# Third attention of a three-layer transformer kernel: another share of gate pieces for each step

## The reference, cut to what matters

```
for each of 8 heads (2 groups of keys, 4 heads each):
    o_c = softmax(q . kc) @ vc        # 31 compressed blocks of keys
    o_s = softmax(q . ks) @ vs        # selected keys: here all of the causal ones
    o_w = softmax(q . kw) @ vw        # window of 256 keys
    o   = g0 * o_c + g1 * o_s + g2 * o_w
out = sigmoid(x @ w_gate_mla) * (o_mla @ w_o_mla) + sigmoid(x @ w_gate_nsa) * (o_nsa @ w_o_nsa)
```

## Time and profile before

| | |
|---|---|
| median of 3 runs | 2529.7 us |
| profiled execution | 2527.73 us, span 2525.9 us |
| PE busy | 2501.9 us, 99% of the span |
| DVE busy | 1386.6 us, 55% |
| ACT busy | 941.4 us, 37% |
| mean granted TensorE clock | 0.998 |
| the NSA attention with its pieces | 1964.4 to 2095.5 us of the span |

### The profile page before, as it was taken

How to read it: one execution, slowest core, us unless ns; L and a number is a source line. 1 busy time by engine, 2 the same in 40 slices (tenths; PEclk the granted TensorE clock), 3 DMA queues, 4 the chain that set the end, 5 groups by cost and what they waited for, 6 DMA issues and landing times.

```text
span 2525.9 us, 29885 instructions
## 1 busy us (share of the span) xinstructions
PE 2501.9 (99%) x11809; PEld 2024.9 (80%) x11809; DVE 1386.6 (55%) x1902; ACT 941.4 (37%) x1359; POOL 60.3 (2%) x77
## 2 busy tenths in 40 slices
PE   9999999999999999999999999999999999999999
PEld 7788888888888877888888888888777658888887
DVE  6556366644556655545664454666655566733433
ACT  5432334322234443223342233445534564422222
POOL 6000000000000000000001000000000001000000
PEclk9999999999999999999999999999999999999999
DMA  4122223444443322222244333222222111222222
GB/s 164 67 84 98 85 100 108 149 143 150 149 143 108 104 67 77 91 101 91 101 142 136 132 104 131 100 92 94 100 101 71 47 34 67 100 100 98 94 91 100
DMA packets 38627, 260.02 MB, mean 103 GB/s; under 512 B 4416, under 2 KB 4672, under 8 KB 8048
## 3 DMA queue, kind: packets, MB, share of 16 engines
q1 hardware_dynamic: 32976, 226.92, 26.4%
q10 hardware_dynamic: 5296, 30.20, 3.4%
q0 software_dynamic: 240, 1.28, 0.2%
HBM read 256.29 MB, written 2.10 MB: 102 GB/s over the span
## 4 chain that ended last, share of the span: by engine, by line
PE 94%; DVE 3%; ACT 1%; issue 1%; DMA 0%; SPq 0%; DVEq 0%; ACTq 0%
PE ps L2043 65%; PE ps L2070 9%; PE ps L2278 6%; PE ps L2096 5%; PE ps L2220 2%; PE ps L2262 2%; PE ps L2242 1%; DVE w_lo L1166 1%; PE ps L2504 1%; PE ps L2520 1%; PE ps L2196 0%; PE ps L2560 0%; PE ps L2366 0%; DMA h<-x_t 0%; ACT pads L686 0%
## 5 line engine op out<-in xcount | busy, mean ns | idle before, releaser
L1166 DVE TENSOR_TENSOR w_lo<-raw,w_hi 128x2048 fp32r<-128x2048 f32 x208 | 477.6, 2296 | 325.0 <-ACT w_hi L598 275.1
L2043 PE MATMUL ps<-a_hi,w_hi 128*128 128x512 f32 x1408 | 550.5, 391 | 0.3 <-DVE w_lo L1166 0.3
L2043 PE MATMUL ps<-a_hi,w_lo 128*128 128x512 f32 x1408 | 547.9, 389 | 0.0
L2043 PE MATMUL ps<-a_lo,w_hi 128*128 128x512 f32 x1408 | 547.8, 389 | 0.0
L598 ACT ACTIVATE w_hi<-raw 128x2048 fp32r<-128x2048 f32 x198 | 376.5, 1901 | 404.2 <-PE ps L2043 338.3
L2043 PEld LDWEIGHTS ps<-a_hi,w_hi 128*128 128x128 f32 x1408 | 264.3, 188 | 56.8 <-issue 1.1
L2043 PEld LDWEIGHTS ps<-a_lo,w_hi 128*128 128x128 f32 x1408 | 264.4, 188 | 55.4 <-issue 1.0
L2043 PEld LDWEIGHTS ps<-a_hi,w_lo 128*128 128x128 f32 x1408 | 264.3, 188 | 55.0
L2043 PE MATMUL ps<-f_hi,w_hi 128*128 128x512 f32 x708 | 275.4, 389 | 0.0
L2043 PE MATMUL ps<-f_lo,w_hi 128*128 128x512 f32 x708 | 275.4, 389 | 0.0
L2043 PE MATMUL ps<-f_hi,w_lo 128*128 128x512 f32 x708 | 275.4, 389 | 0.0
(11 more groups left out here) (387 smaller groups left out, 3544.9 us busy)
## 6 DMA issues: line engine op xcount, KB each, us to landing
raw<-weights SPq DMA_DIRECT2D x209, 1024.0 KB, 4.8
ada_w<-ada ACTq DMA_DIRECT2D x24, 1024.0 KB, 4.9
merged<-cmp_w SPq DMA_DIRECT2D x2, 1024.0 KB, 5.9
out<-h SPq DMA_DIRECT2D x8, 256.0 KB, 2.0
h<-x_t SPq DMA_DIRECT2D x3, 512.0 KB, 7.2
raw<-weights SPq DMA_DIRECT2D x4, 256.0 KB, 5.2
kt<-c_row ACTq DMA_DIRECT2D x2, 512.0 KB, 3.4
pads<-p_t ACTq DMA_DIRECT2D x2, 512.0 KB, 4.1
```

What stands on the lines that cost most here:

```text
L1166: dve.tensor_tensor(w_lo[n % 2][:, w], raw[n % 2][:, w], w_hi[n % 2][:, w].bitcast(F32), ALU.subtract)\
L2043: ins = pe.matmul(dst, a[i], b[j], start=done == 0, stop=done == total - 1)
```

## The change

The list `share` is replaced. The order of the pieces, their number (48) and everything else stay.

```
-                share = [0] + [3, 2, 2, 1, 1, 1, 2] * 3 + [3, 3, 2, 2, 1, 1]
+                share = ([0, 3, 3, 2, 0, 2, 1, 2] + [3, 3, 2, 1, 2, 0, 2] + [2, 2, 2, 0, 2, 1, 1] + [2, 2, 0, 3, 3, 2])
```

## The result

| | before | after |
|---|---|---|
| median, of 5 runs each | 2529.74 us (2528.09 to 2530.45) | 2516.55 us (2515.53 to 2518.67) |
| ratio after / before, 95% interval | | 0.9949 (0.9935 to 0.9964) |
| profiled execution | 2527.73 us, span 2525.9 | 2517.49 us, span 2515.7 |
| first scores of the attention (line 2212) | 1964.43 | 1966.03 |
| first matmul of `out_nsa` (line 2070) | 2095.52 | 2085.31 |

A forecast was written before the change was run, and what follows sets the result against it. TensorE (PE), busy 99% of the span, was taken as the bound. 8.2 + 4.7 + 0.7 - 2.6 = 11.0 us off the 2529.7 us median forecast 2518.7 us; 8-in-10 range 2514.5 to 2524.0.

The forecast's parts named there:

- (a): PE's five waits for ScalarE's gate eviction, at the first pieces of tiles 1 to 5, all go: 8.2 us gained.
- (b): PE's two low-clock stretches, behind the waits at steps 9 and 23, go if those waits cause them: 4.7 us gained.
- the rival that rested on the rule: Clock falls elsewhere, behind new short waits in piece-free steps; one fall costs 3.4 us, giving 2522.1 us; chance 0.13.
- (c): Each group of pieces on PE costs 0.19 us beside its pieces; four groups disappear: 0.7 us gained.
- New waits: PE's waits where pieces no longer cover the chain through VectorE and ScalarE: 2.6 us added, bounds 0 and about 5.
- Steps 4 and 18: Without their piece, the next step's transposes wait for VectorE's weighing: 0.87 us added for each.
- Step 11: At full clock PE arrives sooner and waits for VectorE, which has low weights ahead of its mask: 0.35 us added.
- Steps 19 to 22: ScalarE's `w_hi` and VectorE's `w_lo` delay copies and masks once the gate wait goes: 0.3 us added, bound 1.2.
- The wait at step 9 stays: Tile 1's eviction comes late, so the 1.74 us wait and 3.4 us of low clock stay: 2523.8 us; chance 0.07.
- Cover counts more: New waits reach 5 us, with one clock fall: gain 5.2, 2524.5 us; chance 0.09 for larger waits or two falls.
- Hidden anyway: A later stage held by something other than PE gives the gain back: time stays 2529.7 us; chance 0.03.
- Slower: The clock falls behind every new wait, five places at 3.4 us each: 2535.7 us; chance 0.02.

The follow-up runs named there:

- 1: Changed kernel with the border at step 9 put back: tile 1 ends in the step where tile 2 begins; 2518.4 us, ratio 0.9957.
- 2: Kernel before with only the border at step 9 mended: step 8 has 4 pieces and ends tile 1; 2524.87 us, ratio 0.9988.
- 5: Kernel before with only the border at step 23 mended, tile 4 ending there and step 24 left empty; 2524.7 us.
- 6: Kernel before with only the border at step 23 mended, without an empty step, tile 5 beginning in step 24; 2523.29 us.
- 8: Changed kernel with only the border at step 23 put back (4 pieces there, 1 in step 25); 2522.69 us, ratio 0.9973.
- 3: Changed kernel with one piece given back as cover to steps 4 and 18, from steps 5 and 19; 2515.81 us, ratio 0.9951.
- 4: Changed kernel, same tile borders, with all empty steps but 24 filled with pieces from other steps; 2516.93 us, ratio 0.9954.
- 7: Changed kernel with one piece moved from step 5 to step 4 and one from step 10 to step 11; 2515.77 us, ratio 0.995.
- 11: Kernel 4's list, but with the weight-unit splits kept at steps 1, 9 and 19, as in the changed kernel; 2515.95 us, ratio 0.9944.
- 12: Kernel 4's list with weight-unit splits at fixed steps 1, 9 and 24, the third moved from step 19; 2514.22 us, ratio 0.9943.
- 9: Changed kernel with the borders at steps 9 and 23 both put back; 2522.87 us, ratio 0.9972.
- 10: Kernel before with its old list, but ScalarE's gate eviction placed ahead of the exponentials of step s+2; 2521.91 us, ratio 0.9974.

## Why the prediction was right

**(a) The gate waits: right.** 8.2 us forecast and 8.2 gone, the border at step 9 with it. Kernels 1, 2, 5, 6 and 8 show that each of the two borders within a step makes its own wait, and that this wait goes when the tile ends with its step. Slack at step 9 was put at 1.6 us and is 1.7.

**(b) The clock: right in this profile, as a mechanism only in part.** The step reads "if the low clock follows from the two long waits, both losses go with them: 4.7 us". In the stage there is no fall in any of the six kernels without a gate wait (after, 3, 4, 7, 11, 12), and every fall in the stage goes with one of the two long waits. (In before at tile 5 the clock is down from 2076.90, 0.3 us ahead of the end of the wait, and so before TensorE works again.) But the wait alone doesn't decide it. In the profiles, before's own included:

```
wait of PE            profiles with it            clock fell behind it
1.74 us, tile 2       before, 1, 5, 6, 9          before, 5, 6
2.4 to 3.5 us, tile 5 before, 2, 8, 9, 10         before, 8, 9, 10
0.55 to 1.23 us       13 waits (before, 2, 5, 6, 10)  none
```

A fall cost 1.7 or 3.4 us. So the two waits bring a chance of a fall in each execution, not a certain 4.7 us. The 62 executions of the kernel before in the four jobs show the same thing (mean granted clock, number, lowest, median and highest us):

```
0.996   6   2531.70   2532.27   2532.74
0.997  34   2528.61   2529.60   2531.46
0.998  16   2527.07   2527.88   2528.50
0.999   4   2525.68   2525.78   2526.55
1.000   2   2523.26             2523.35
```

The spread of 9.5 us between runs of one kernel goes with the clock. After's five runs are at 0.999 (2516.55 to 2518.67) and 1.000 (2515.53 and 2515.55). At 1.000 the difference of the kernels is 2523.3 - 2515.5 = 7.8 us, against 8.2 + 0.7 - 2.6 = 6.3 by the prediction's terms without the clock (7.4 with the sizes measured below). The rest of the 13.2 us, some 5 us, goes with the clock. This is rough: 0.001 of mean clock is 2.5 us of the span, and only two runs of each stand at 1.000.

The Trainium skill's rule (TensorE: Matmul & The Clock Gate, section "A second HAM failure mode: psum-queue depth-cycling"), by which short idles make the clock swing, is borne out in the stage for waits from 1.7 us, by 7 of 10 in the table. It is not for those up to 1.23 us there: neither the old gate waits nor the five waits of after, up to 0.95 us, brought a fall. But this is no length that holds everywhere. At the kernel's start, behind the wait of line 2162 at 25 to 26 us (the same work in all fourteen profiles), a fall of 1.7 us came in seven of them:

```
wait in us (profile it was in)
fall      0.92 (8)  1.16 (6)   1.39 (4)  1.63 (1)       1.67 (11)  1.81 (2)  1.83 (after)
no fall   0.83 (3)  0.87 (12)  1.03 (5)  1.25 (before)  1.32 (9)   1.43 (7)  1.61 (10)
```

PE's timeline there and the window behind it, of kernel 8:

```profile
25.13 1.05 PE L2162 MATMUL ps<-consts_sb,pads 128*128 128x1 f32 x8 [0.92 <-DVE pads L1238]
```

```profile
25.00:30.00 5.00, 4.87 (x19) 4.01 (x20) 3.25 (x12) 3.07 (x4) 4.42 (x8) 0.66 0.02 5
```

In the other direction, a wait of 1.5 us near 1791 us stands in all fourteen profiles and no fall follows it. So the rival that rested on the rule did not come in the stage, but the argument that I held against it, that 1.23 us or less brings no fall, does not hold for this kernel as a whole.

**(c) The price of a group: wrong.** 0.7 us were forecast and nothing came. The four steps that lost their group took as long as before, less the pieces and waits (the ledger of the stage). Kernel 7 confirms it: it has one group more than after, its waits are 0.67 us shorter, and its stage is 0.67 us shorter. The step counted a group from the start of its first piece, and did not look at what the transposes ahead of it cost when no piece follows.

**New waits: right in kind, 0.6 us too high.** Steps 4 and 18 cost 0.89 - 0.19 = 0.70 and 0.71 us. I had 0.87 each, since I counted the price of a group here too; without it PE arrives 0.7 us early. Step 11: 0.38 - 0.19 = 0.19 against 0.35. Steps 19 to 22: 0.22 against 0.3. Step 23: 0.21 against 0.2. Steps 13 and 24: 0, as said. Together 2.0 against 2.6.

**The sum.** 11.0 us were forecast for the profiled execution, and the stage gave 11.8. That it came so near is in part luck, since three wrong sizes offset each other. The 0.7 us of (c) did not come, and the new waits were 0.6 us too high by the same mistake. Left out was what a gate wait costs beyond its brackets, 0.22 to 0.26 us where it can be read (steps 5, 15 and 19; step 9 by kernel 1), an estimate of 1.2 us for five. For the clock 5.0 - 0.4 = 4.5 us are left, against 4.7. With these sizes the sum is 8.2 + 1.2 + 4.5 - 2.0 = 11.9. Then 1.6 us were lost again at the kernel's start, by a fall that the change has nothing to do with, so `out_nsa` starts at 2085.31 and not at 2084.5. The falls near 25 to 32 us are in seven of the thirteen profiles of after and the experiments (after, 1, 2, 4, 6, 8, 11). The median came 2.2 us below the forecast. 0.8 us of it is the stage. The rest is probably that the forecast was made from an execution at 0.998, while the kernel before ran at 0.997 or below in 40 of 62 executions, with more clock to give back.

**The rivals.** The wait at step 9 stays: refuted by the trace of after; kernel 1 shows its price, 1.9 us and perhaps a fall. Cover counts more: refuted by after, whose new waits are 2.0 us and not 5. Giving the cover back shortened the stage by 0 to 0.7 us (kernels 3, 4 and 7), and by 1.3 to 1.9 us once the splits stayed behind (11 and 12). Hidden anyway: refuted by the median. Slower: no new wait brought a fall.

**Open.** What decides in one execution whether a wait of 1.7 to 3.5 us is followed by a fall of 0, 1.7 or 3.4 us. Neither its length nor the place settles it, as kernels 1 and 9 against before, 5 and 6 show, and 2 against before; nor does the length settle it at the kernel's start. It is also not known why the wait of line 2162 there varies between 0.83 and 1.83 us, and no run shows that it is this wait that brings the fall.

## What to carry to other kernels

When one buffer is handed from tile to tile, look at the step in which both the last work of the old tile and the first of the new one stand, and count in the evicting engine's program what lies ahead of the eviction. Moving the border takes a piece from one place and can uncover a chain there (0.6 us of new waits in kernel 2, 0.9 in 5 and 6, against 1.7 and 3.5 us gained). An empty step behind the border costs the cover that its work gave (0.7 us in each of steps 4 and 18, nothing in 13 and 24), and what it saves can be small (0 to 0.3 us in kernel 4). A tile that ends with its step is not safe for that alone: compare the end of the eviction with the time at which the next tile wants the buffer. To price a group of work, compare the steps with it and without it from the same start to the same start, and not the group alone. Before moving a piece of work, list everything that is tied to it (here 1.9 us of ScalarE's split with the first piece of a unit): tied work can take back the whole gain, and in the profiles untying it (kernels 11 and 12) was worth more than any further shift. A wait of TensorE can have a second price, a fall of the clock. It came in some executions only, so it must be counted over several of them.

## What the runs showed of the hardware

The kernel before, on one core, took between 2523.3 and 2532.7 us in 62 runs, and this spread followed the mean granted clock (1.000 to 0.996). Both ends of it were measured on the same chip. The same wait, 1.74 us at the same instruction, was followed by 3.4, 1.7 or 0 us lost in different profiled executions, and one of 3.52 us by none (kernel 2). In the stage waits of 1.23 us and less were never followed by a fall. At the kernel's start falls of 1.7 us came behind waits from 0.92 to 1.83 us in seven of fourteen profiles, and near 1791 us a wait of 1.5 us was followed by none in any. A gate wait cost 0.22 to 0.26 us more than its brackets show. A group of pieces had no price of its own (1.73 us with it and 1.72 without, in step 4).
